# Expert loads issued without waiting for the ones before, the second router loaded later, the first weight tile in quarters

## What is computed

```python
for layer in range(2):
    if layer == 0:
        x = x + sgu_mixer(rmsnorm(x, a_norm), ...)        # gelu(h @ w_in + b_in), mixing of positions, @ w_out
    else:
        k, v, cum = shared_kv(x, kv_norm, kv_w, ...)      # x after layer 0
        x = x + forgetting_attention(rmsnorm(x, b_norm), k, v, cum, b_w_qg, q_norm, b_w_out)
    x = x + hierarchical_moe(rmsnorm(x, m_norm[layer]), ...)

def hierarchical_moe(h, w_group, ..., w1, w3, w2):        # 32 experts, 2 for each of 512 positions
    # per expert e and its rows xb:
    return (silu(xb @ w1[e]) * (xb @ w3[e])) @ w2[e]
```

## Time and profile before

| | |
|---|---|
| median of 3 runs | 1641.7 us (1637.36 to 1642.05) |
| the profiled execution's own time | 1638.44 us |
| its span, first to last instruction | 1636.7 us |
| PE busy | 1499.2 us, 92% of the span |
| moved by DMA | 462.14 MB, mean 282 GB/s |

### The profile page before, as it was taken

The page is one execution under the profiler, slowest core; times in us unless marked ns, Lnnn a source line. Parts: engine busy times, 40 slices in busy tenths (PEclk is TensorE's granted clock), DMA queues, the critical chain, the costliest instruction groups (busy, mean ns, idle before and its releaser), DMA issues.

```text
span 1636.7 us, 45535 instructions
## 1 busy us (share of the span) xinstructions
PE 1499.2 (92%) x18893; PEld 1007.2 (62%) x18894; DVE 982.1 (60%) x2067; ACT 459.3 (28%) x759; POOL 25.8 (2%) x63
## 2 busy tenths in 40 slices
PE   8999999999899899987799999999999999977667
PEld 7888888755455455544678754468665556544334
DVE  5336642477677577754734446752777777754446
ACT  5442221422122122211532434534122222211111
POOL 3100000100000000000000000000000000000000
PEclk9999999999999999998899999999999999998888
DMA  5421223899999999999231321234899997999995
GB/s 208 133 103 52 103 103 118 338 364 414 412 414 414 427 429 420 414 429 422 82 103 52 117 77 31 86 149 198 362 414 420 407 429 316 410 429 428 428 428 210
DMA packets 55656, 462.14 MB, mean 282 GB/s; under 512 B 4432, under 2 KB 4560, under 8 KB 31024
## 3 DMA queue, kind: packets, MB, share of 16 engines
q1 hardware_dynamic: 51680, 453.00, 67.5%
q10 hardware_dynamic: 2192, 4.23, 0.8%
q0 software_dynamic: 1728, 4.11, 0.8%
HBM read 459.19 MB, written 2.13 MB: 282 GB/s over the span
## 4 chain that ended last, share of the span: by engine, by line
PE 67%; DMA 26%; DVE 4%; issue 1%; SPq 0%; ACT 0%; DVEq 0%
DMA EB<-in_m_w 26%; PE ps L1358 12%; PE ps L1214 9%; PE ps L1216 9%; PE ps L1215 9%; PE ps L1347 6%; PE ps L1368 6%; PE ps L1330 4%; PE ps L1601 3%; PE ps L1586 1%; PE ps L1614 1%; PE ps L1627 1%; PE ps L1210 1%; PE ps L1457 1%; PE ps L1237 1%
## 5 line engine op out<-in xcount | busy, mean ns | idle before, releaser
L1358 PE MATMUL ps<-EB,SCR 128*32 128x256 f32 x6016 | 374.2, 404 | 96.4 <-DMA EB<-in_m_w 82.6
L1358 PEld LDWEIGHTS ps<-EB,SCR 128*32 128x32 f32 x6016 | 198.7, 116 | 264.4 <-issue 141.0
L925 DVE TENSOR_TENSOR X<-X,ps 128x1024 f32 x188 | 221.1, 1218 | 28.7 <-PE ps L1330 28.7
L1216 PE MATMUL ps<-EB_r 128*128 128x512 f32 x512 | 199.6, 390 | 0.0
L1347 PE MATMUL ps<-H,SCR 128*32 128x256 f32 x3072 | 185.8, 382 | 0.0
L917 DVE TENSOR_TENSOR SCR<-SCR,ps 128x128 f32<-128x128 f32 x94 | 36.9, 392 | 245.4 <-ACT SCR L629 245.3
L1368 PE MATMUL ps<-EB,SCR 128*32 128x256 f32 x3008 | 179.7, 379 | 0.0
L632 ACT ACTIVATE SCR_r<-ps,SCR 128x256 f32 x94 | 44.5, 473 | 445.6 <-PE ps L1368 445.6
L1368 PEld LDWEIGHTS ps<-EB,SCR 128*32 128x32 f32 x3008 | 98.9, 110 | 63.5
L1330 PEld LDWEIGHTS ps<-SCR_r 32*128 32x128 f32 x3136 | 100.5, 185 | 48.0 <-issue 42.1
L1347 PEld LDWEIGHTS ps<-H,SCR 128*32 128x32 f32 x3072 | 90.1, 109 | 62.2
(11 more groups left out here) (239 smaller groups left out, 1619.9 us busy)
## 6 DMA issues: line engine op xcount, KB each, us to landing
EB<-in_m_w SPq DMA_DIRECT2D x192, 2048.0 KB, 9.9
EB<-in_a_w_in SPq DMA_DIRECT2D x8, 2048.0 KB, 9.1
EB<-in_a_w_out SPq DMA_DIRECT2D x4, 2048.0 KB, 7.9
EB<-in_kv_w SPq DMA_DIRECT2D x4, 2048.0 KB, 14.2
EB<-in_b_w_qg SPq DMA_DIRECT2D x4, 2048.0 KB, 8.0
EB<-in_b_w_out SPq DMA_DIRECT2D x2, 2048.0 KB, 9.1
X<-in_x SPq DMA_DIRECT2D x4, 512.0 KB, 6.9
SCR<-ncum_rows ACTq DMA_DIRECT2D x8, 256.0 KB, 3.9
```

The lines of the kernel that those rows point to most:

```text
L925: add = v.tensor_tensor(X_t, X_t, moved[1][:, :, t, :], ALU.add)
L1216: return mm(o, left[1], right[0], start=False, stop=stop)
L1358: last = mm(ps[0][g * CAP:(g + 1) * CAP, 0:2 * P].rearrange("p (w n) -> p w n", w=2), xT[:, k, :], w13_sb[s][:, :, k, g * P:(g + 1) * P], ...
```

## The change

Six edits in three groups. (1) `load_later_expert` no longer waits for the landing of the previous expert's matrices; the waits for `up` and `down` stay. In layer 0 the load of w1 of expert 1 is issued at `out_done` 14 instead of after 16. (2) POOL issues the norm vector of the attention layer first, and the second router's four loads and its scaling behind it, instead of in the first expert items of layer 0. (3) The first weight tile comes as four transfers of 512 KB with a semaphore each; ACT rounds its quarters between the transposed blocks 1 and 2 and the blocks 2 and 3; and the 16 products on constants after the last transpose are gone.

```diff
-            def load_later_expert(l, e, s, before, loads_before):
+            def load_later_expert(l, e, s):
                 m = moe[l]
-                sp.wait_ge(m["w13"][before], 32 * loads_before)
                 ended = sp.value_load(n0_i[0:1, bass.ds(e - (NBUF - 1), 1)], min_val=1, max_val=MAX_ITEMS)
                 sp.wait_ge(m["up"], ended)
...
                 sp.dma_start(w1_sb[s], w1e).then_inc(m["w13"][s], 16)
-                sp.wait_ge(m["w2"][before], 16 * loads_before)
                 sp.dma_start(w3_sb[s], w3e).then_inc(m["w13"][s], 16)
                 sp.wait_ge(m["down"], ended)
                 sp.dma_start(w2_sb[s], w2e).then_inc(m["w2"][s], 16)
...
-                load_expert(l, 1, (1, 3) if l == 0 else (3,))
+                load_expert(l, 1, (3,))
...
-            load_tile(0)
+            for q in range(4):
+                sp.dma_start(ring[0][:, 2 * q:2 * q + 2, :], tiles[0][:, 2 * q:2 * q + 2, :]).then_inc(first_loaded[q], 16)
             load_tile(1)
...
             load_expert(0, 1, (2,))
+            sp.wait_ge(out_done, 14)
+            load_expert(0, 1, (1,))
             sp.wait_ge(out_done, 16)
             moe_loads(0)
...
-            pool.wait_ge(tile_loaded[0], 16)
+            pool.wait_ge(first_loaded[3], 16)
...
-            pool.wait_ge(moe[0]["xg"], 1)
+            pool.wait_ge(norm["kv"]["hrow"], NT)
+            load_gain("b", b_norm[0])
             load_router(1)
             scale_router(1)
-            pool.wait_ge(norm["kv"]["hrow"], NT)
-            load_gain("b", b_norm[0])
...
+            def split_first(q0, q1):
+                for q in range(q0, q1):
+                    act.wait_ge(first_loaded[q], 16)
+                    a.activation(ring_hi[0][:, 2 * q:2 * q + 2, :], ring[0][:, 2 * q:2 * q + 2, :], ACT.Copy)\
+                        .then_inc(w_hi, 1)
...
-            transposed_rows("a")
-            split_tile(0)
+            for t in range(NT):
+                turned_hi("a", t)
+                if t in (1, 2):
+                    split_first(2 * t - 2, 2 * t)
...
-                keep_busy(1, (0, 4, 6, 16)[t])
+                keep_busy(1, (0, 4, 6, 0)[t])
```

More of the change, by code:

```diff
@@ L225, in trunk @@
         tile_loaded = sems("tile_loaded", 2)
+        first_loaded = sems("first_loaded", 4)
         w_hi = sem("w_hi")
@@ L398, in moe_loads @@
                     for s in range(NBUF):
-                        load_later_expert(l, r * NBUF + s, slot(s), slot(s - 1), r + (1 if s else 0))
+                        load_later_expert(l, r * NBUF + s, slot(s))
                 for e in range(NE // NBUF * NBUF, NE):
-                    load_later_expert(l, e, slot(e), slot(e - 1), (e - 1) // NBUF + 1)
+                    load_later_expert(l, e, slot(e))
             for t in range(NT):
                 sp.dma_start(X[:, t, :], x_in[0, t * P:(t + 1) * P, :]).then_inc(x_loaded[t], 16)
-            load_tile(0)
+            for q in range(4):
+                sp.dma_start(ring[0][:, 2 * q:2 * q + 2, :], tiles[0][:, 2 * q:2 * q + 2, :]).then_inc(first_loaded[q], 16)
             load_tile(1)
@@ L594, in split_tile @@
             def split_tile(i, q0=0, q1=4):
-                split_hi(i % 2, i // 2 + 1, q0, q1)
+                split_hi(i % 2, i // 2 + i % 2, q0, q1)
             def moe_act(l, ready):
@@ L653, in _ @@
                         if t == 0:
-                            split_hi(1 - j, r + 1 + j)
+                            split_hi(1 - j, r + 1)
             act.wait_ge(wsts_ready, 1)
@@ L1593, in _ @@
                     if i == 0:
-                        pe.wait_ge(tile_loaded[j % 2], 16 * (j // 2 + 1))
+                        pe.wait_ge(tile_loaded[j % 2], 16 * (j // 2 + j % 2))
                         if c >= 1:
```

## The result

The changed kernel takes **1623.81 us**, the median of 4 runs (1622.16 to 1626.14). The kernel before took 1641.88 beside it (4 runs, 1637.36 to 1645.38). The ratio is 0.9893, with a 95% interval of 0.9865 to 0.992. Measured a second time beside other variants it was 0.9909 (0.9875 to 0.9943). Over all measurements of this study before has 90 runs (median 1639.4, from 1631.5 to 1653.8) and after has 10 (median 1625.3): 14.1 us apart, where I had forecast 13.4. The profiled execution of after took 1626.14 (span 1624.4), 12.3 less than that of before.

What follows compares the result with a forecast made beforehand. Outside the experts PE's own work was taken to bound the kernel, inside them PE and DMA in turns. Gains 3.4 + 9.4 + 1 - 0.4 = 13.4 us, from 1641.7 to 1628, range 1622 to 1637.

Steps and rivals of the forecast that it cites:

- The start: Kernel start: quartered weight tile and no constants let PE's first real product begin at about 16.3 instead of 19.67, gaining 3.4 us.
- the constants' clock: Kernel start: constants might be needed to keep TensorE's clock; the prediction counted nothing for their removal.
- Experts of layer 0: Expert loads of layer 0: earlier issues and a higher transfer rate together gain 9.4 us.
- The head start: Layer 0, experts 3 and 4: w1 issued sooner, so the load queue runs 5.4 us ahead.
- The rate: Layer 0, first twelve experts: transfers follow without the excess of 0.45 us per period, gaining 4 us more, bounds 0 and 5.
- 425 GB/s or more in the window of the first twelve experts: Layer 0 expert loads: DMA rate the profile after should show, against 412 GB/s if the rate did not improve.
- The prediction's cap from item 2: Layer 0: expert 4's w1 must await PE's item 2, issued at 348.47, which cuts the queue's lead to 5.4 us.
- Experts of layer 1: Layer 1 expert loads: no lasting lead, but a cleaner queue shortens one wait by about 1 us, bounds 0 to 3.
- The router's loads: Layer 0 expert stretch: moving the second router's 0.16 MB, 0.4 us at 427 GB/s and off the path, gains 0.
- POOL's scaling: Router scaling on POOL, moved beside DVE's splitting of a weight tile: 0.4 us lost, between 0 and 0.8.
- the rate stays: Rival, chance 0.26: the expert loads' lower rate has a cause SP does not touch; gain 8.4 us, 1633.3.
- a deeper queue is a slower queue: Rival, chance 0.05: up to eight outstanding expert transfers hinder each other; gain gone, or slower at about 1653 us.

Runs made afterwards that it cites:

- const0_only: The kernel before without the constant products behind the last transposes, first weight tile still one transfer: 1640.66 us, ratio 1.0008.
- later_issue: The kernel before with the item's number read three times instead of once ahead of each later expert's w1 issue: 1685.41 us, ratio 1.0277.
- only_w1_free: The kernel before without w1's landing wait, w3 still waiting for w2 of the expert before: 1631.18 us, ratio 0.996.
- after_three_reads: The changed kernel with the item's number read three times ahead of each w1: 1625.22 us, ratio 0.9902 to the kernel before.
- after_again: The changed kernel, unchanged, measured once more beside other variants: 1627.22 us, ratio 0.9909 to the kernel before.
- nowait_only: The kernel before with only the two landing waits of the expert loads left out: 1630.61 us, ratio 0.9928.
- early_w1_only: The kernel before with only w1 of expert 1 issued at out_done 14, landing waits kept: 1635.52 us, ratio 0.9982.
- moe_both: The kernel before without the landing waits and with the early w1 of expert 1, old start and router place: 1628.88 us, ratio 0.9944.
- after_const16: The changed kernel with the constant products behind the last transposes put back: 1630.13 us, ratio 0.9936 to the kernel before.

## Why the prediction was right, by its own steps

**The start, 3.4 forecast: 4.05 measured.** The four landings were forecast at 11.7, 13.1, 14.4 and 15.8 and came at 11.7 to 15.7. The order on ACT and DVE was as told: ACT's quarters end at 14.13, DVE starts at 14.01. What I had too small is that the transposes themselves end 0.47 sooner (14.83 against 15.30), as the first eight constants took 1.43 us instead of 1.92, and the first product overlaps the last transposes by a quarter of a microsecond. The first of these is no part of the change: the first product of kernels with the old start varied from 18.72 to 19.98, that of the five with the new start and no constants from 15.58 to 16.20. So 4.05 is the difference of one pair. It was carried to item 0 whole (3.99). I gave the constants' clock nothing. For after that holds, since nothing idles there; the claim without the quarters would have been wrong, as `const0_only` shows. The Trainium skill, "DMA: Bandwidth & Descriptors", section "Anatomy of one DMA", has a fixed cost of about 2 us for each transfer. It fitted that to transfers that GpSimd issues, and does not say that queued ones pay it one after the other; these are SP's. Queued behind each other the pieces came about 1.35 apart ((15.7 - 11.7)/3), so here the fixed part overlaps, as the prediction had it from X's pieces.

**Experts of layer 0, 9.4 forecast: 10.4 measured** (last item's up products at 755.60 instead of 770.04, so 14.4, less the start's 4.0). Its two terms:

- The head start, 5.4. Expert 3's issue was forecast at 326.2 (325.61), expert 4's near 345 (343.69). Landing 7.6 behind its issue, the latter came at 351.3; in before 361.4. That is 10.1, of which 4.0 is the start: 6.1. The prediction let item 2 move with the start alone; it came another 0.8 sooner (18.07 behind item 0 instead of 18.86).
- The rate, 4. The late w1 landings of experts 5 to 14, 4.6 us in before, are gone in all six traces without landing waits, but for one of 0.3. The cause that I read, an issue with too little left in the queue, is shown by `later_issue`, `only_w1_free` and `after_three_reads` together; it is not the whole cause (see what stays open). That its size fits is luck: it was read from one execution, and in others with w1's wait the lateness was 0.3 to 4.3 in layer 0. The sign "425 GB/s or more in the window of the first twelve experts" did not come as written (418, and 428 only from 352 on). After's own traces differ as well: in `after_again` layer 0's last item is 7.4 sooner, the start taken off, not 10.4, while its whole time is the shorter one (1623.39).

The two terms don't simply add to the parts measured alone. `nowait_only` has 10.0 us and `early_w1_only` 5.1, but both have 9.7, since the head start of each is cut off at the same place: w1 of expert 4 answers item 2 of PE in both (348.76 and 348.00, and 349.16 with both). The prediction's cap from item 2 is that.

**Experts of layer 1, 1 forecast: about 0.** From layer 1's first item to its last, before took 456.1 us, the two traces of after 456.6 and 455.3, and `after_three_reads` 455.1. The queue is cleaner (6 late landings of 3.0 us in before, one at most in after), and PE's one wait before 1410, at item 9, fell from 3.2 to 2.4 and 1.8 in two traces. What it wins there can go again by the clock: in the first of these traces the products behind that wait took 5.35 instead of 3.66, in the second 3.66. The step was off by its size, within its own bounds (0 to 3).

**The router's loads, 0 forecast: 1.6 when alone.** This step failed as put: "they were 0.16 MB, 0.4 at 427 GB/s, off the path". They were on the path, since the landing wait of expert 3's w1 hung on the last prefetch, and they took 1.9 us of the queue's time. In after no weight of the step can be seen: with the old place (`moe_both`) item 24 stands 212.7 behind item 0, with the new one 211.8 in after and 213.0 in `after_const16`. That this is because w1 no longer waits for that landing is argued.

**POOL's scaling, 0.4 lost forecast: none seen.** It runs at 797.36 for 0.67 us, over the end of a DVE instruction and 0.2 us of the first split of a weight tile:

```profile
797.36 0.67 POOL L497 TENSOR_TENSOR wr<-wr,cols 128x288 f32<-128x288 f32 x1 [2.58 <-DMA br<-in_m_b_expert]
...
797.85 2.40 DVE L814 TENSOR_TENSOR EB_r<-EB,EB_r 128x1024 fp32r<-128x1024 f32 x2
```

The pair takes 2.40, where two at the start took 4.62/2 = 2.31; after's lead over before is 14.4 at 755 and 14.5 at 1126. By the Trainium skill, "SBUF — State Buffer", section "Who interferes with whom", the two would exclude each other. An overlap of 0.2 us is too short to show that, so this case leaves the rule open.

**The sum.** 3.4 + 9.4 + 1 - 0.4 = 13.4 against 12.3 in the first pair of profiled executions and 14.1 over all runs. In that pair the start and layer 0 gave 14.4, 1.0 more than all the terms together; the stretch between the layers took back 1.6, nearly all of it the slow constants, and layer 1 some 0.5. So the sum is closer than its terms: the start and layer 0 were too small, layer 1 too large, and that they cancel is luck. The first measurement's medians, 18.1 apart, have before at the high side of its own scatter. The 1628 was reckoned from 1641.7, the median of three runs; from the 1639.4 of all 90 the same 13.4 gives 1626.0, against 1625.3 measured. The rival "the rate stays" would have needed w1 to come late after the change too; "a deeper queue is a slower queue" would have needed landings over 4.89 apart with up to eight outstanding. Neither is in any trace.

**What stays open.** Before's runs spread over 22 us, after's 10 over 6. Late landings differ from execution to execution (14, 16, 9, 9, 11, 5 of 20 in the six kernels with both landing waits and one read), which would spread the time, and `only_w1_free` and those without waits spread less on the whole (2.8 to 10.5 us against 7.8 to 20.2, of 4 to 12 runs each). But no execution at 1650 was profiled, so that its time is lost there is only argued.

The margin of 4.05 us alone doesn't make a w1 late. In before itself w1 of experts 15 to 22 of layer 0 is issued with the same margin, and all eight land on time. What goes with it is how far the DMA engines are out of step. A transfer reports its landing in sixteen signals, taken here as one for each DMA engine, and the traces keep their times. In the six traces with both landing waits and one read, a w1 issued 3.9 to 4.35 us ahead was late 10 times in 173 where the signals of the transfer ahead of it came within 1.4 us of each other, 33 times in 80 where they took 1.4 to 2.0, and 33 times in 40 where they took longer. Experts 5 to 14 are where they took long. In the kernels without w1's wait they lay as far apart there (1.7 to 3.1 us), and next to nothing was late. By these counts it takes both, engines out of step and a short margin, which is close to what the prediction read, engines that run ahead of the others. It is counted over traces and not tested by a run, and at 2.9 us it does not hold: in `later_issue` all 26 were late where the signals lay within 2.0 us, and 10 of 26 where they lay further apart. What puts the engines out of step stays open.

## What to carry to other kernels

In a stretch bound by DMA, look at when each transfer is issued against the time at which the queue would run dry, and not only whether the queue runs dry. A wait that throttles the queue to one transfer ahead leaves a margin that everything behind it on the issuing engine eats up, and here one microsecond of it was worth 47 us. Where constants keep PE busy while data come, they and the data's arrival are one step: take them out only together with the wait that they cover.

## What the runs showed of the hardware

- A 2 MB transfer in a queue that never runs low lands 4.89 us behind the one before, nearly without scatter, with up to eight outstanding. In experts 5 to 14, issued 4.88 us or more ahead of its turn (w3 in the kernels with waits) it was late 0 to 2 times in 20; issued 4.05 ahead 5 to 16 times in 20, by 0.1 to 1.6 us; issued 2.9 ahead 14 times in 20, by up to 2.5. In experts 15 to 31 4.05 us was nearly always enough (late 13 times in 171).
- At 4.05 us ahead the lateness goes with how far apart the sixteen landing signals of the transfer ahead lie: late 10 times in 173 within 1.4 us, 33 times in 40 beyond 2.0.
- Reading a number from SBUF into a register of SP and waiting on it puts 0.82 us between a landing and the next issue; two reads more put 1.1 us on top.
- Four small loads on POOL's queue (0.16 MB together) delayed the 2 MB transfers beside them by 1.9 us in the one pair of traces compared, about five times their share by bytes.
- After 3.03 us of idle PE at the start the granted clock of the window from 20 to 40 us was 0.91; in the thirteen traces without that idle time it was 1.00. The same 20 products on constants took 2.50 us in one execution of after and 3.92 in another, at a granted clock of 0.61, with the same program.
